# Where the tiles lie in SBUF: the 64 KB shared by the stages moved from the top to the bottom

## The reference, cut to what matters

```
for l in range(2):
    h = modulate(rmsnorm(x), sh1, sc1)
    x = x + 0.5 * g1 * swiglu(h, ffn1_w_in[l], ffn1_w_out[l])      # 1024 -> 2*2816 -> 1024
    h = modulate(rmsnorm(x), sh2, sc2)
    x = x + g2 * token_mixing(h, ...)   # 3 mixers, gates, merge, w_out
    h = modulate(rmsnorm(x), sh3, sc3)
    x = x + 0.5 * g3 * swiglu(h, ffn2_w_in[l], ffn2_w_out[l])
return rmsnorm(x)
```

## The kernel before, in words

| tile | bytes a partition | address before | address after |
|---|---|---|---|
| x | 16384 | 16512 | 82048 |
| uh | 16384 | 32896 | 98432 |
| ul | 16384 | 49280 | 114816 |
| raw | 24576 | 65664 | 131200 |
| wh | 12288 | 90240 | 155776 |
| wl | 12288 | 102528 | 168064 |
| ada_raw | 8192 | 114816 | 180352 |
| ab_hi, ab_lo | 256, 256 | 144992, 145248 | 210528, 210784 |
| ssq, sq | 2048, 4096 | 151040, 153088 | 216576, 218624 |
| A0: hh, oh | | 157184 | 16512 |
| hl | 24576 | 181760 | 41088 |
| ol | 16384 | 173568 | 32896 |
| end | | 222720 | 222720 |

## Time and profile before

### The profile page before, as it was taken

The page is one execution under the profiler, slowest core; times in us unless marked ns, Lnnn a source line. Parts: engine busy times, 40 slices in busy tenths (PEclk is TensorE's granted clock), DMA queues, the critical chain, the costliest instruction groups (busy, mean ns, idle before and its releaser), DMA issues.

```text
span 2611.2 us, 36437 instructions
## 1 busy us (share of the span) xinstructions
PE 2483.8 (95%) x11908; PEld 2013.1 (77%) x11908; DVE 1336.3 (51%) x1500; ACT 890.9 (34%) x1271; POOL 1181.5 (45%) x1683
## 2 busy tenths in 40 slices
PE   3999999999999999999989999999999999999998
PEld 2888887788777778888878888877887777788886
DVE  7443446766466754434444434376664666433333
ACT  3431233422255434322344222243223554442232
POOL 6877774734344417777227777147224342000000
PEclk9999999999999999999989999999999999999999
DMA  7443442322324523433324434232222344232221
GB/s 279 149 145 121 144 147 99 119 85 77 112 70 141 170 97 131 167 114 137 111 90 145 153 113 151 99 109 93 81 90 90 114 153 136 81 104 97 86 103 61
DMA packets 90713, 310.99 MB, mean 119 GB/s; under 512 B 11568, under 2 KB 11952, under 8 KB 90480
## 3 DMA queue, kind: packets, MB, share of 16 engines
q1 hardware_dynamic: 57888, 215.87, 23.5%
q0 software_dynamic: 18896, 68.56, 7.6%
q10 hardware_dynamic: 13824, 25.17, 2.8%
HBM read 294.88 MB, written 14.68 MB: 119 GB/s over the span
## 4 chain that ended last, share of the span: by engine, by line
PE 86%; DVE 7%; issue 3%; ACT 3%; DMA 0%; SPq 0%; DVEq 0%; ACTq 0%
PE PS L430 72%; PE PS L442 3%; PE PS L823 1%; PE PS L635 1%; PE PS L646 1%; PE PS L649 1%; DVE wl L1179 1%; DVE up_m L1591 1%; DVE ada L1617 1%; ACT wh L876 1%; PE PS L596 1%; ACT sco L1066 0%; PE PS L702 0%; PE PS L698 0%; PE PS L713 0%
## 5 line engine op out<-in xcount | busy, mean ns | idle before, releaser
L1179 DVE TENSOR_TENSOR wl<-raw,wh 128x1024 fp32r<-128x1024 f32 (+2 forms) x360 | 570.5, 1585 | 856.4 <-ACT wh L876 855.8
L430 PE MATMUL PS<-uh,wh 128*128 128x512 f32 x2144 | 860.3, 401 | 15.8 <-DVE wl L1179 12.5
L430 PE MATMUL PS<-uh,wl 128*128 128x512 f32 x2144 | 838.8, 391 | 0.0
L430 PE MATMUL PS<-ul,wh 128*128 128x512 f32 x2144 | 838.8, 391 | 0.0
L383 POOL TENSOR_TENSOR ada_raw<-ada_raw 128x512 f32<-128x512 f32 (+9 forms) x1280 | 734.1, 574 | 100.2
L876 ACT ACTIVATE wh<-raw 128x1024 fp32r<-128x1024 f32 (+2 forms) x360 | 401.5, 1116 | 900.7 <-PE PS L430 872.6
L430 PEld LDWEIGHTS PS<-uh,wh 128*128 128x128 f32 x2144 | 404.5, 189 | 112.7 <-DVE wl L1179 15.7
L430 PEld LDWEIGHTS PS<-uh,wl 128*128 128x128 f32 x2144 | 404.0, 188 | 85.7
L430 PEld LDWEIGHTS PS<-ul,wh 128*128 128x128 f32 x2144 | 404.9, 189 | 80.7 <-issue 2.9
L373 POOL DMA_DIRECT2D ada_raw<-in_ada_w_dram x128 | 71.9, 562 | 742.7 <-PE PS L430 388.6
L379 POOL TENSOR_TENSOR ada_raw<-ada_raw,cond 128x1024 f32<-128x1024 f32 x128 | 321.0, 2508 | 103.8 <-DMA ada_raw<-in_ada_w_dram 92.1
(11 more groups left out here) (226 smaller groups left out, 2245.9 us busy)
## 6 DMA issues: line engine op xcount, KB each, us to landing
raw<-in_ffn_in_dram SPq DMA_DIRECT2D x176, 512.0 KB, 3.2
ada_raw<-in_ada_w_dram POOLq DMA_DIRECT2D x128, 512.0 KB, 3.8
raw<-in_mix_in_dram SPq DMA_DIRECT2D x88, 512.0 KB, 3.3
raw<-in_ffn_out_dram SPq DMA_DIRECT2D x32, 768.0 KB, 4.3
raw<-in_ffn_out_dram SPq DMA_DIRECT2D x32, 640.0 KB, 3.8
g_in<-gates_dram ACTq DMA_DIRECT2D x48, 256.0 KB, 4.1
ada<-in_ada_w_dram SPq DMA_DIRECT2D x16, 512.0 KB, 10.7
raw<-in_mix_up_dram SPq DMA_DIRECT2D x16, 512.0 KB, 3.3
```

What stands on the lines that cost most here:

```text
L430: mm = e.matmul(PS[:, bank, :], w[:, j % 2, k * P:(k + 1) * P], v[:, k, :], start=(k == 0 and w is wh and v is xh), stop=(k == K - 1 and w ...
L1179: TTo(wl[:, j % 2, 0:K * P], raw[:, j, 0:K * P], wh[:, j % 2, 0:K * P], ALU.subtract)\
```

## The change

A0 is taken first, at 16512, and the running address then starts 65536 higher. No instruction, order, shape or semaphore changes. Every tile outside the 64 KB is 65536 bytes higher than before, and every tile inside them is 140672 bytes lower.

```diff
             return nc.alloc_sbuf_tensor_at(name, shape, dt, offset=off)
+
+
+        A0 = base[0]
+        base[0] += 65536
 
         x = place("x", [P, KD, SEQ], F32)
...
         sq = place("sq", [P, 2, SEQ], F32)
-        A0 = base[0]
         h32 = place("h32", [P, 2, SEQ], F32, A0 + 57344)
...
-        assert A0 + 65536 <= 229368, A0 + 65536
+        assert base[0] <= 229368, base[0]
```

## The result

| | before | after |
|---|---|---|
| median, us (lowest, highest) | 2615.77 (2609.83, 2619.98), 4 runs | 2596.40 (2593.26, 2598.26), 4 runs |
| span of the profiled execution, us | 2611.2 | 2593.9 |

The ratio is 0.9927, with a 95% interval of 0.9910 to 0.9945: 19.4 us less, where 14.8 was forecast. Timed again beside the last group of experiments, the changed kernel gave 0.9937 (0.9920 to 0.9953), that is 16 us. In the kernel after, the lines named here are three higher: L433 is the old L430, L826 the old L823.

A forecast was written before the change was run, and what follows sets the result against it. The prediction took the pace of the L430 matmuls on TensorE to bound the kernel. Savings of 13.9 us (hh, hl) and 0.9 (oh, ol), the rest 0, gave -14.8 us, from 2616.5 to 2601.7 us, range 2593 to 2622.

The forecast's parts named there:

- Step 1: FFN matmuls with hh or hl moving: 2112 step at 226.7 ns instead of 233.3, 13.9 us saved.
- Step 2: Branch projections (L823, oh and ol moving): 2.5 us less TensorE work, of which 0.9 counts, bounds 0 and 2.5.
- The sign I had named: L823's stage: it shrinks by 0.5 us and DVE's share of its chain grows.
- Step 3: Matmuls with uh or ul moving: cost 0, the 480 of the input projection still take 108.6 us.
- k = 1: L540's weight slice at 128 modulo 256 like uh: about 224 ns a matmul against 230 to 233, favouring low bits.
- Step 4: DVE and ACT on the moved tiles: no effect of the address, 0; DVE stays at 693 ns, ACT at 632.
- Step 5: DMA, first ada loads to A0 at the start: 0, with 0.5 us either way.
- B: Rival: weights and moving operand in different SBUF halves cost 6.6 ns; hh stays slow, uh slows, 2660 us; chance 0.13.
- The other reading: Within the forecast case: a moving operand above 131072 is slow by itself, whatever its low address bits.
- A: The forecast: low address bits, or the moving operand's half alone, decide the matmul pace; 2601.7 us, 2594 to 2608; chance 0.67.
- C: Rival: the change doesn't touch the cause of hh's slow pace; 2616.5 us, 2610 to 2621; chance 0.20.

The follow-up runs named there:

- e4: The kernel before with hh and hl alone 128 bytes higher, oh and ol left at 0: 2601.51 us, ratio 0.9949.
- e1: The kernel before with A0 128 bytes higher, so hh, hl, oh, ol stay above 131072 but lie at 128 modulo 512: 2594.87 us, ratio 0.9932.
- m1: Microbenchmark, no kernel: groups of 48 fp32r matmuls with chosen weight and moving addresses; 226.7 ns a step at difference 0, 232.5 at 128.
- e3: The kernel before with all tiles 384 bytes higher and A0 another 128, so weights and moving operands all lie at 0 modulo 512: 2598.97 us, ratio 0.9938.
- e7: The kernel before with wh and wl 128 bytes higher, at 0 modulo 256 like hh and oh, while uh and ul stay at 128: 2634.77 us, ratio 1.0076.
- a2: The changed kernel itself, unaltered, timed again beside the last group: 2599.66 us, ratio to before 0.9937.
- e5: The kernel before with A0 128 bytes higher but hh and hl kept where they were: 2610.85 us, ratio 0.9978.
- e2: The changed kernel with A0 384 bytes higher and other tiles 512 higher, so hh, hl, oh, ol are low but at 0 modulo 512: 2615.25 us, ratio 0.9999.
- m2: The microbenchmark with finer address differences, other column counts and data types; fp32r with 512 moving columns never below 226.7 ns, slowest 239.1.

## Why the prediction was right

The forecast of 2601.7 us is 5.3 above the 2596.40 measured. Of that, 2.5 is in the span (2596.4 forecast, 2593.9 measured) and 2.8 in the offset from span to median, which I had carried over as 5.3 and which came out as 2.5. The range, 2593 to 2622, took in no change at all, so it is the stretches that show the mechanism and not the time alone.

**Step 1, hh and hl.** Right in mechanism and size. The forecast gave 65.1 and 54.2 us for the two halves, and 65.06 and 54.17 came. 2112 x 6.6 = 13.9 us; e4, which does this alone, measured 13.3 (9 to 18).

**Step 2, oh and ol.** Right in direction, too small in size: forecast 0.9 us for the two stages together, measured 0.70 and 0.75, 1.45 in all (46.79 to 46.10 in the first). The saving of 1.27 us a stage came through by a little over half, and not by the 36% that TensorE had of the chain there: the share of a chain was a poor measure of what a faster TensorE saves. The sign I had named failed as well. DVE's share of the chain did not grow, it fell from 38% to 32%; what took TensorE's place is the gates' way back from HBM. The chain after, by line and two of its pieces (start us, us, what):

```profile
by line: DMA g_in<-gates_dram 29.1%; issue 21.4%; DVE up_m L1594 18.1%; PE PS L826 12.4%; DVE up_m L1598 7.4%; ACTq L1102 3.4%; DVE up_m L1602 3.1%; ACT g_in L1135 2.6%; DVE ul L1585 2.4%; DVE wl L1182 0.5%; DVEq L1181 0.2%; DVEq L1592 0.1%
...
839.89 5.74 PE PS L826 x24
848.42 7.31 DMA g_in<-gates_dram
```

**Step 3, uh and ul.** Right: 108.57 us for 480 matmuls, against 108.59, though the weights are now high and uh low. e1 and m1 too show that no half of SBUF costs anything. L540's first matmuls of each k start as in the earlier trace rows, here at 469.09, 469.78, 470.46, 471.15: 0.69, 0.68, 0.69 us. The rounding of the earlier trace rows had made the difference too large. From unrounded starts the kernel before has 695, 678, 694 and 693 ns for k = 0 to 3, so 226 a matmul at k = 1 and 231 elsewhere, 15 to 17 ns on three matmuls and not 20 to 30. The dip at k = 1 stands in both layers of all eight traces in which k = 1 has equal starts modulo 256, among them e3, where both lie at 0 and not at 128. Two runs speak less clearly for the reading. In e7, where equal starts fall on k = 5, only the first layer has a dip there (686 ns; 697 in the second), and in m1's copy of the pattern k = 1 takes 686 and then 692 ns among slices of 686 to 699. So equal starts are a fitting reading of k = 1 and not a shown one. m1's copy shows the same 231.4 ns in the mean with the weights in either half. Why the third matmul of a k is short stays open.

**Step 4, DVE and ACT.** Right: hl 691 ns at least and 693 in the median, hh 632, ssq 691 and 693 after as in the earlier trace rows.

**Step 5, the start.** Forecast 0 with 0.5 us either way, measured -1.4 us: a term missed by mechanism. The first loads take slightly longer with A0 at 128 modulo 256 (11.0 us to landing in the median, against 10.7 in the earlier trace rows); so it is in all nine traces of whole kernels, 10.9 to 11.0 in the four with A0 at 128 and 10.6 to 10.7 in the five with it at 0. DVE's small scale_eff comes 0.05 us later, and an overlap with GpSimd's multiplication is gone. DVE in the kernel before:

```profile
37.71 2.48 DVE L1201 SCALAR_TENSOR_TENSOR scale_eff<-ada_sum,norm_g 128x8 f32<-128x8 f32 x1 [0.15 <-DVE ada_sum L1621]
```

and GpSimd beside it:

```profile
37.80 2.35 POOL L379 TENSOR_TENSOR ada_raw<-ada_raw,cond 128x1024 f32<-128x1024 f32 x1
```

In the kernel after, DVE and then GpSimd:

```profile
37.76 0.17 DVE L1204 SCALAR_TENSOR_TENSOR scale_eff<-ada_sum,norm_g 128x8 f32<-128x8 f32 x1 [0.15 <-DVE ada_sum L1624]
```
```profile
38.37 3.14 POOL L382 TENSOR_TENSOR ada_raw<-ada_raw,cond 128x1024 f32<-128x1024 f32 x1
```

An operation of 0.17 us took 2.48 and ended with the GpSimd operation beside it, which ended at 40.15. The nine traces bear out that the overlap does it. In before, e3, e4 and e7 GpSimd's operation starts 0.09 to 0.16 us behind scale_eff, within its 0.17, and scale_eff takes 2.48 to 2.54 us. In after, a2, e1 and e5 it starts 0.57 to 0.70 behind, in e2 0.22, and scale_eff takes 0.17. DVE and GpSimd in e2:

```profile
37.67 0.17 DVE L1204 SCALAR_TENSOR_TENSOR scale_eff<-ada_sum,norm_g 128x8 f32<-128x8 f32 x1 [0.15 <-DVE ada_sum L1624]
```
```profile
37.89 2.36 POOL L382 TENSOR_TENSOR ada_raw<-ada_raw,cond 128x1024 f32<-128x1024 f32 x1
```

All four traces with A0 at 128 modulo 256 are free of the overlap, and e2 with A0 at 0 is too, by a hair. So it hangs on the timing of two queues; that the later landings are what shifts GpSimd is likely and not shown. Part of the 2.3 us comes back: the two wl<-raw,wh behind it take 4.51 us together where they took 3.90.

**The sum.** The span fell by 17.3 us. By stages, from the starts of first matmuls in both traces: 14.5 in the eight stages with hh, the last with the closing norm included, 1.5 in the branch stages, 1.4 at the start, and 3.7 in the first input projection (137.98 to 134.24 us), whose steady pace is unchanged; the remaining stages give 3.8 back. The prediction had no term for either of these two. In the first output projection of the mixer more time was at half clock (granted clock, 1.00 to 0.96). Before and after:

```profile
46.49:184.47 137.98, 134.10 (x576) 0.99 0.40 140
897.31:942.53 45.22, 43.71 (x192) 1.00 0.30 104
```
```profile
45.13:179.37 134.24, 132.50 (x576) 1.00 0.40 142
886.22:934.17 47.95, 45.30 (x192) 0.96 0.28 98
```

In the first input projection TensorE waits less for the third weight unit, and the stretch at half clock behind that wait (granted clock 0.97 from 40 to 90 us, against 1.00 after) is gone. Its first L430 behind the wait, before and after:

```profile
63.34 0.79 PE L430 MATMUL PS<-uh,wh 128*128 128x512 f32 x1 [3.85 <-DVE wl L1179]
```
```profile
59.76 0.50 PE L433 MATMUL PS<-uh,wh 128*128 128x512 f32 x1 [1.73 <-DVE wl L1182]
```

The traces of after, a2 and e1, in which hh and all else of the 64 KB lie at 128 modulo 256, have the short wait (1.73 us in each) and gain 3.3 to 3.7 us in this stage; the other six wait 2.8 to 4.5 us. So the gain may belong to the change, and may be why after, a2 and e1 gained 16 to 19 us and e3 and e4 13 to 16. With one traced execution a run, and no cause known, that is not shown.

The terms whose mechanism the traces show come to 14.5 + 1.5 + 1.4 = 17.4. That this is nearly the 17.3 of the spans is luck, since 3.7 and -3.8 cancel. What the 19.4 of the medians has beyond it lies inside its interval, 14.4 to 23.5 us.

**The rivals.** B (weights and moving operand in different halves) is refuted by the changed kernel itself, where hh is low, wh high and the step 226.7 ns, and by m1. The other reading, which A took in, that a moving operand above 131072 is slow by itself, is refuted by e1 (high and fast) and e2 (low and slow). C (nothing happens) fell with the result. The Trainium skill's rule on the two independent read ports ("TensorE: Matmul & The Clock Gate", "Part 2: What happens when you issue a matmul"), as the prediction read it, would have given no change. Its figure of about 216 ns at 512 columns is what m2 shows for bfloat16, 215.9 ns, the same at the three differences tried. For fp32r at 512 columns the runs disagree: 226.7 ns at best and up to 239.1, by the start of the weights against that of the moving operand. What in the chip makes it so, no run here shows.

## What to carry to other kernels

Where fp32r matmuls with 512 moving columns bound a kernel, start weights and moving operands at the same offset modulo 256, and at multiples of 32: here 128 bytes of padding were worth 0.6 to 0.7%. In m2 operands that both started 4 bytes off were the slowest, 12 ns over 227; no whole kernel was tried so. To find such a thing, compare the step from start to start of the same instruction form on different tiles, in stretches where TensorE has no gap and the clock is 1.00; a mean duration dilutes it. A change of layout that seems to be about a region may be about its low bits, so test the region and the bits apart.

## What the runs showed that I had not expected

- The cost depends on the operands' starts in a way that fits no simple picture of mine: period 256, fast at differences of 0, 16 and 240, slow at 4, 8, 12, at all tried from 20 to 224 and at 248. Between differences 0 and 128 there is no effect with 256 moving columns (120.0 ns), in float32 (429.2) or in bfloat16 (215.9).
- At a good difference, 64 and 32 weight columns are slower (230.1 and 231.9 ns) than 128 or 8 (226.7 and 226.8).
- Steps in the slow case are not uniform: with hh in the kernel before they alternate 229 and 238 ns for whole stretches. In the kernel after they are 226 and 227, also with hh, and after a disturbance they come back to that within ten steps.
